# Another order of VectorE's work in the first stage of a two-block model: the modulation row's parts, the score weighting and the pooling trade places

## What is computed

```
mod = silu(c) @ ada_w + ada_b            # six rows of 1024: shift, scale, gate, twice
h = rms_norm(x) * (1 + scale_a) + shift_a
proj = h @ w_in                          # columns u, v, o, i, f, p
y_m = mlstm(u, v, o, i, f)               # 4 heads of 128: conv, q, k, decay weights, gated output
y_p = pool(p)                            # 4 groups of 128 channels, windows 2, 4, 8, 16
x = x + gate_a * (concat(y_m, y_p) @ w_out)
# then: norm, 32-expert layer, and the second block (gated MLP, SwiGLU, attention, SwiGLU)
```

## Time and profile before

| | before |
|---|---|
| time, median of 3 runs | 2123.7 us |
| time of the profiled execution | 2123.7 us |
| its span | 2121.9 us |
| PE busy | 1972.6 us (93%) |
| DVE busy | 1199.0 us (57%) |
| ACT busy | 967.5 us (46%) |
| POOL busy | 192.2 us (9%) |

### The profile page before, as it was taken

The page is one execution under the profiler, slowest core; times in us unless marked ns, Lnnn a source line. Parts: engine busy times, 40 slices in busy tenths (PEclk is TensorE's granted clock), DMA queues, the critical chain, the costliest instruction groups (busy, mean ns, idle before and its releaser), DMA issues.

```text
span 2121.9 us, 22807 instructions
## 1 busy us (share of the span) xinstructions
PE 1972.6 (93%) x8886; PEld 1585.0 (75%) x8886; DVE 1199.0 (57%) x1542; ACT 967.5 (46%) x1467; POOL 192.2 (9%) x247
## 2 busy tenths in 40 slices
PE   4999969999999999879999999998899989999997
PEld 3757757777778777648888888887676768888886
DVE  7676688888888888753543333334344443333323
ACT  2433167887878888624232222124345433222221
POOL 3200120122001110020000000001010110000000
PEclk8999879999999999989999999999999999999999
DMA  8454369999999999742332323222111104323311
GB/s 277 139 168 162 124 241 347 358 349 368 348 360 343 353 339 347 271 144 78 101 98 80 103 96 99 90 90 82 40 60 60 60 30 147 109 82 100 100 40 40
DMA packets 195609, 361.90 MB, mean 171 GB/s; under 512 B 13429, under 2 KB 79738, under 8 KB 195498
## 3 DMA queue, kind: packets, MB, share of 16 engines
q1 hardware_dynamic: 179520, 337.66, 46.3%
q10 hardware_dynamic: 5818, 11.98, 1.5%
q0 software_dynamic: 10160, 10.74, 1.5%
HBM read 364.52 MB, written 20.97 MB: 182 GB/s over the span
## 4 chain that ended last, share of the span: by engine, by line
PE 87%; DVE 7%; DMA 2%; issue 2%; ACT 2%; SPq 1%; POOL 0%; ACTq 0%; DVEq 0%; POOLq 0%
PE ps L263 84%; DVE wlo L210 2%; DMA raw<-in_w_in 1%; PE ps L1920 1%; DVE GM L1993 1%; PE ps L720 1%; SPq L874 1%; DMA raw<-in_w_expert_gate 0%; DVE wlo L214 0%; ACT whi L191 0%; DMA raw<-in_w_expert_down 0%; PE ps L2471 0%; DVE hT5l L260 0%; DVE widelo L2739 0%; DVE widehi L2739 0%
## 5 line engine op out<-in xcount | busy, mean ns | idle before, releaser
L210 DVE TENSOR_TENSOR wlo<-raw,whi 128x1024 fp32r<-128x1024 f32 (+1 forms) x576 | 672.1, 1217 | 327.6 <-ACT whi L191 323.1
L191 ACT ACTIVATE whi<-raw 128x1024 fp32r<-128x1024 f32 (+1 forms) x576 | 573.0, 1047 | 239.9 <-PE ps L263 220.0
L263 PE MATMUL ps<-hT5h,whi 128*128 128x512 f32 x352 | 137.8, 392 | 6.3 <-DVE wlo L210 6.3
L263 PE MATMUL ps<-hT5h,wlo 128*128 128x512 f32 x352 | 137.7, 391 | 0.0
L263 PE MATMUL ps<-hT5l,whi 128*128 128x512 f32 x352 | 137.7, 391 | 0.0
L263 PE MATMUL ps<-hT3h,whi 128*128 128x512 f32 x352 | 137.0, 389 | 0.6 <-DVE hT3l L260 0.6
L263 PE MATMUL ps<-hT3h,wlo 128*128 128x512 f32 x352 | 136.9, 389 | 0.0
L263 PE MATMUL ps<-hT3l,whi 128*128 128x512 f32 x352 | 136.9, 389 | 0.0
L2336 DVE TENSOR_TENSOR tmpT<-tmpT,ps 128x512 f32<-128x512 f32 x44 | 30.1, 684 | 139.3 <-PE ps L263 139.3
L263 PE MATMUL ps<-whi,XT0h 128*128 128x512 f32 x256 | 102.1, 399 | 1.9 <-DVE XT0l L1944 1.9
L263 PE MATMUL ps<-whi,GTh 128*128 128x512 f32 x256 | 100.8, 394 | 1.7 <-DVE GTl L1997 1.7
(11 more groups left out here) (425 smaller groups left out, 4080.0 us busy)
## 6 DMA issues: line engine op xcount, KB each, us to landing
raw<-in_w_expert_gate SPq DMA_DIRECT2D x64, 1024.0 KB, 8.4
raw<-in_w_expert_up SPq DMA_DIRECT2D x64, 1024.0 KB, 8.6
raw<-in_w_expert_down SPq DMA_DIRECT2D x64, 1024.0 KB, 6.8
raw<-in_ffn_w_gu SPq DMA_DIRECT2D x44, 1024.0 KB, 5.1
raw<-in_ffn_w_down SPq DMA_DIRECT2D x20, 1024.0 KB, 5.0
raw<-in_ada_w SPq DMA_DIRECT2D x32, 512.0 KB, 4.8
raw<-in_w_in SPq DMA_DIRECT2D x8, 1024.0 KB
raw<-in_a_w_in SPq DMA_DIRECT2D x8, 1024.0 KB, 8.7
```

The lines of the kernel that those rows point to most:

```text
L191: e.activation(hi[:, c], raw[:, c], ACT.Copy).then_inc(self.S("w_hi"), 1)
L210: e.tensor_tensor(lo[:, c], raw[:, c], hi[:, c].bitcast(F32), ALU.subtract).then_inc(self.S("w_lo"), 1)
L263: return e.matmul(o, l, r, start=start, stop=stop, skip_group_check=True)
```

## The change

Only `first_sync` and `first_vec` are edited. No instruction is added, removed or changed in size; DVE's calls between `masked(1)` and the first `mix_low` stand in another order, and two of SP's weight loads move behind two more loads of parts.

```diff
             for m in range(32):
-                W.load(e, {2: 6, 4: 7, 8: 8, 18: 9, 22: 10, 24: 11, 28: 12}.get(m, 0))
+                W.load(e, {2: 6, 4: 7, 8: 8, 18: 9, 24: 10, 26: 11, 28: 12}.get(m, 0))
...
             masked(0)
             masked(1)
+            ada_parts(e, own, 4, 5)
             weigh(0)
-            ada_parts(e, own, 4, 5)
             W.low(e, W.index["o"][1] + 1)
+            ada_parts(e, own, 6, 7)
             key(2)
             masked(2)
             weigh(1)
-            ada_parts(e, own, 6, 7)
+            ada_parts(e, own, 8, 9)
             key(3)
             masked(3)
-            weigh(2)
-            ada_parts(e, own, 8, 9)
+            ada_parts(e, own, 10, 11)
             pooled(0)
             pooled(1)
-            ada_parts(e, own, 10, 11)
             ada_parts(e, own, 12, 13)
+            weigh(2)
+            ada_parts(e, own, 14, 15)
             pool_out(0)
             e.wait_ge(S("pool_sum"), 4)
             e.memset(VN[:, :, :, P:P + 1], 1.0).then_inc(S("v_one"), 1)
+            pooled(2)
             pool_out(1)
-            weigh(3)
-            ada_parts(e, own, 14, 15)
-            pooled(2)
             pooled(3)
             W.low(e, W.index["v"][0] + 1)
             ada_parts(e, own, 16, 17)
+            weigh(3)
+            ada_parts(e, own, 18, 19)
             pool_out(2)
             pool_out(3)
-            ada_parts(e, own, 18, 19)
+            ada_parts(e, own, 20, 21)
             W.low(e, W.index["v"][1] + 1)
-            ada_parts(e, own, 20, 21)
-            W.low(e, W.index["wo"][0] + 1)
             ada_parts(e, own, 22, 23)
...
+            W.low(e, W.index["wo"][0] + 1)
             for gi in range(4):
                 mix_low(4 + gi, PT[:, gi, 16:528], gi + 1)
```

## The result

The changed kernel takes 2141.6 us (median of 7 runs, 2138.9 to 2152.3) against 2124.7 for the kernel before in the same comparison (7 runs, 2118.9 to 2130.5): a ratio of 1.0087, 95% interval 1.0063 to 1.0111. By the medians it is slower by 16.9 us (the interval says 13 to 24); the forecast was 15.9. Its profiled execution took 2137.1 us with a span of 2135.4.

A forecast was written before the change was run, and what follows sets the result against it. The prediction took PE, held where it waits for DVE, to bound the edited stretch; 3.1 + (6.1 - 3.1) + (13.4 - 6.1) + 2.5 = 15.9 us on 2123.7 gave 2139.6, range 2131 to 2149.

The forecast's parts named there:

- Third group, bank, weighting: PE's third score group takes the bank the same head's weighting frees; a weighting x later holds PE x later.
- Head 0: Parts 4 and 5 ahead of the weighting of head 0 make PE 3.1 us later (bounds 2.1 to 4.0).
- brush with POOL: Parts 4 and 5 meet POOL's additions; one wait for DVE, 1.0 us (bounds none to 1.9).
- Head 2: Parts 10 to 13 and two poolings ahead of its weighting; PE 6.1 us late at unit `o` 2.
- Head 3: List from `pool_out(0)` ahead of its weighting, 9.1 us; PE 13.4 late at unit `o` 3, new hole about 7.
- The second loss of clock: PE's clock falls behind a second hole too, adding 2.5 us (bounds 0 to 7.5).
- The sum: All terms together make PE 15.9 us late, giving 2139.6 us.
- The cover: Low parts of `v` 1 and first `wo` covered by PE's lateness: cost 0, or 2.3 us for one if not.
- The distance holds to the end: Sign of being right: `v` starts about 16 us later and the same distance holds to the end.
- Larger: Rival: loads land in 7.4, each part meets POOL, clock stays low longer; 24 us, 2148; chance 0.14.
- smaller: Rival: DVE and POOL don't meet, loads land in 3.7, clock holds; 11.3 us, 2135; chance 0.14.
- Not slower: Rival: PE not held by the weighting, hole before unit `o` 2 shrinks to 2.7; 2119 to 2121.5 us; chance 0.06.

The follow-up runs named there:

- e5: Changed kernel, DVE's order untouched, scores given three PSUM banks instead of two; 2124.1 us, ratio 0.9988 to the kernel before.
- e9: Kernel before with only the weighting of head 3 moved late, behind parts 16 and 17; 2143.1 us (one run).
- e2: Changed kernel with the weighting of head 2 back directly behind the masking of head 3; 2138.5 us (one run).
- e3: Changed kernel with the weighting of head 3 back ahead of the pooling of group 2; 2137.8 us (one run).
- e4: Changed kernel with the weightings of heads 0, 2 and 3 all back in their old places; 2129.1 us, ratio 1.0015 to the kernel before.
- e11: Kernel before with three score banks and nothing else; 2126.0 us, ratio 1.0.
- e7: Kernel before with poolings 0 and 1 ahead of parts 6 and 7 and ACT's sigmoid of unit `o` 0 moved up; 2130.1 us, ratio 1.0019.
- e8: Kernel before with early poolings and sigmoid, low part of `v` 1 and joins earlier, parts 24 to 31 later, one weight load moved up; 2126.5 us, ratio 1.0002.

## Why the prediction was right, step by step

*Third group, bank, weighting.* Right, and shown from both sides: taking the bank away as the reason (e5) removes the loss with DVE's order untouched, and moving one weighting alone (e9) makes one of 13.9 us at `v`.

*Head 0.* Forecast 3.1, measured 2.8: unit `o` 0 started at 106.84 for 104.03. The brush with POOL was 0.7 (3.27 for 2.6), I had taken 1.0. The Trainium skill, SBUF — State Buffer, section Who interferes with whom, has this as an exclusive lock; the rows of both engines agree with it in kind, DVE 0.7 and POOL 1.8 us longer. But it did not add the 0.9 that I had worked out from it. They took turns: part 4 was first (102.56) and held up POOL's addition, that addition held up part 5 (1.96 us), and part 5 held up POOL's next one. So POOL waited twice and DVE once.

*The clock behind the first hole.* Not foreseen. Unit `o` 1 started 4.4 us late, not 3.1: the clock fell after a hole of 2.65 us as well, and that cost 1.5 (the stretch at 0.76 above). In e2 and e3, with the same instructions up to there, it did not fall; this 1.5 is not a fixed price of the change.

*Head 2.* Forecast 6.1, measured 7.6 (140.50 for 132.94). The weighting started at 139.11, which is 1.2 behind the forecast, and that is PE's lateness from head 0 (4.4 for 3.1), with which the masking of head 3 begins; the parts, their loads and the poolings took what was worked out for them. (The lower bound of this term was mis-added: landings of 3.7 give 5.2, not 5.0.) The rest is PE's own pace after the hole (0.66 from the group to the unit for 0.35).

*Head 3.* Forecast 13.4, measured 14.5 (159.65 for 145.13); it follows from head 2, and the list from `pool_out(0)` on was priced right: 9.1 forecast, and from 149.47, where `pool_out(0)` began, to 158.25 it took 8.8.

*The second loss of clock.* Forecast 2.5, measured 1.2 behind head 3: its unit took 6.96 us for 5.78. With the 1.5 at head 0 that is 2.7 where 2.5 was forecast: the size came out right and half of it lay elsewhere.

*The sum.* At `v` 15.9 was forecast and 15.7 measured. The two misses on the clock (1.5 not foreseen, 1.3 too much) offset each other, and so do smaller ones: head 0's brush and head 3's list came out 0.3 us shorter each, PE's start behind the two long holes 0.3 longer each. That the sum came out within 0.2 is luck and no merit of the steps; that it came out near 16 is theirs.

*The cover.* I had named two low parts as late but covered, at a price of 2.3 us if not. The cover is real: with PE less late the low part of `v` 1 costs 2.63 (e3) and 2.86 us (e4). The 2.3 was the length of one low part; what PE waits for is made by the loads of the parts ahead of it. Together with what else the list moves, the share was 3.8 us at the experts. So it was rightly left out of the sum, and it would have been the whole answer had the weightings stayed.

*The distance holds to the end.* Nearly: 15.7 at 203 and 216 us (203.13 to 218.83, 216.19 to 231.87), 16.9 at the first expert product (318.97 for 302.04), as the clock stays low for longer in between. In the two profiled executions 13.5 are left at the end. About one of the missing 3.4 us goes at a load of expert weights on the chain, which is longer in the kernel before (8.65 us at 349.30 for 7.88 at 365.88); behind it the distance is 15.8 (362.79 to 378.61). The others go at the end of the expert stage, where the distance falls from 15.7 to 13.4 (946.24 to 959.62): PE's granted clock was 0.67 and 0.81 there in the execution of before (891 to 899 and 913 to 923 us), and 0.80 and 1.00 in the same places of the other. Both run the same instructions there, so I don't put this down to the change; the medians stand 16.9 apart.

*The rivals.* *Larger* and *smaller* did not come. *Not slower* is what happens where the third bank exists, as e5 shows. Its premise, that the 0.17 us are a usual start delay, is answered by e11: with the bank free the same scores take 0.25 us less.

## What to carry to other kernels

A wait of 0.17 us in the weight loads says that a buffer is handed over just in time; whatever is put ahead of the instruction that frees it arrives on the bound engine in full. Ask of each such reader which bank it frees and who stands behind that, and try one more bank before another order. And removing one hole of an engine that waits for another doesn't give back its length: here the next late producer took over part of it (e3), most of it (e2) or all of it (e7, e8), so follow the time to the next stage before counting a gain. Before a difference of 1 to 3 us between two traces is explained by their lists, compare the granted clock in the same stretch of both.

## What the runs showed of the hardware

Equal holes had unequal effects on TensorE's clock. After 2.65 us of waiting the granted clock was 0.76 over the next 7 us in the changed kernel and 1.00 in e2 and e3, whose instructions up to that point are the same; after 2.83 us in e5 it was also 1.00. The rows of the stretch behind the hole, first of e2 and then of e5:

```profile
107.00:114.00 7.00, 6.96 (x28) 5.37 (x29) 6.19 (x6) 0.00 (x0) 1.61 (x2) 1.00 0.57 159
```

```profile
131.00:138.00 7.00, 7.00 (x28) 5.20 (x29) 5.76 (x7) 2.49 (x3) 0.00 (x0) 1.00 0.65 206
```

In the changed kernel eight matmuls came every 0.43 us there, the pace of 1.2 GHz, and then every 0.23. So the price of a short hole beyond its own length was 0 or 1.5 us in runs of the same order, and no single trace decides which. Longer holes vary too: from unit `o` 2 behind the same 4.92 us to the scores of head 3 PE took 9.97 us in the kernel before (132.94 to 142.91) and 8.98 in e2 (136.33 to 145.31). What makes the difference stays open; it wasn't tried.
